# Product-key experts: one product of 512 columns for two of 256, with the halves added by VectorE

## The chip, the cores and the metric

The kernel runs on one core of a Trainium2 chip. The core has five engines that run apart and meet at semaphores: TensorE (PE, matrix products into the eight PSUM banks of 512 columns of float32), VectorE (DVE), ScalarE (ACT), GpSimd (POOL) and SyncE (SP, which here issues the loads). Each engine works through its own instructions strictly in order, and an instruction may wait for a count of a semaphore. The metric is the time of one execution on the device in microseconds; less is better. Inputs, outputs and sums are float32.

## The reference, cut to what matters

The whole program is two transformer blocks: attention of three kinds and product-key experts in the first; a recurrent mixer, latent attention, cross attention and a mixture of experts in the second. The change touches the product-key experts alone:

```python
def peer_ffn(h, w_q, sub1, sub2, u, v):          # h: 256 tokens x 1024
    ...                                          # 8 heads pick 16 of 128 x 128 experts for each token
    expert = jnp.take_along_axis(cand_idx, pos, axis=-1)
    gate = jax.nn.softmax(top_s, axis=-1)
    def step(args):
        x_c, e_c, g_c = args
        a = jnp.einsum('cd,ced->ce', x_c, u[e_c])
        w = jax.nn.gelu(a.astype(jnp.float32), approximate=False).astype(x_c.dtype) * g_c
        return jnp.einsum('ce,ced->cd', w, v[e_c])
```

## The kernel before

The kernel does not gather experts. It walks through all 16384 of them in 128 steps, called keys here, of 128 experts each. For a key it computes the product of the key's `u` (128 experts x 1024) with the input of all 256 tokens, takes gelu, multiplies by a table of gates (zero where a token did not choose the expert), and adds the product with the key's `v` (128 x 1024) to the output, which stays in banks 0 to 3 for all 128 keys.

TensorE gets its operands in a format called fp32r here, which is rounded. To keep precision each operand is split into two parts, high (the rounded value, written by ACT with a copy, `high`) and low (the rest, by DVE with a subtraction, `low`). A product is then three products: high x high, high x low and low x high. The input of the tokens is split once ahead of the loop (`peer_experts`, L1299 to L1313, tiles `peer_input_high` and `peer_input_low`); `u` and `v` of each key in the loop, and the gated values too (`gate`, L1388).

The work of a key n, and who does it:

- SP loads `u` and `v` of the key (512 KB each) into two buffers each (`reload`, L1424). It asks for `v` of key n + 2 when `v_low` of key n is done, and right behind that for `u` of key n + 3, whose condition, `u_low` of key n + 1, is met long before.
- ACT: gelu out of the bank (`act_gelu`, L1364), `v_high`, `u_high`.
- DVE: gate (three operations of 128x256: `gated_high`, `gated`, `gated_low`), `v_low`, `u_low`.
- PE: `pre` (L1328), 8 chunks of 3 matmuls of 256 columns into the first half of one of the banks 4 to 7, and `post` (L1342), 12 matmuls of 512 columns into banks 0 to 3.

The order is written out by hand and shifted, so that engines work on different keys at a time. In its step n PE does `pre` of key n + 2 and then `post` of key n. ACT does gelu of n + 1, `v_high` of n + 1, `u_high` of n + 3 (`act_step`, L1401). DVE does the gate of n + 1, `v_low` of n + 1, `u_low` of n + 3 (`dve_step`, L1413). `v_high` and the gate of a key use buffers that `post` of two keys earlier has read, so they wait for it. A loop (`Fori`) holds four keys in its body, since the banks repeat after four; the first and last four keys stand outside it.

Of the kernel before, what the change touches and what calls it, by code (L numbers as in the profile page):

```python
# [232 lines left out]
class Kernel:  # L233
    def __init__(self, nc, dram, ctx):
# [18 lines left out]
        self.norms_spread = signal("norms_spread")  # L253
        self.scores_ready = signal("scores_ready")
# [1036 lines left out]
def peer_experts(k, gates, raw, hT_keep):  # L1291

    nc = k.nc
    with ExitStack() as c, ExitStack() as c2:
        hT_high, hT_low = (k.sb(f"peer_input_{n}", [P, DC, S], F32R, ctx=c) for n in ("high", "low"))  # L1299

        parts = [[k.sb(f"{m}_{n}", [P, 2, D], F32R, ctx=c) for n in ("high", "low")] for m in "uv"]
        hT = k.sb("peer_input_T_again", [P, DC, S], ctx=c2)
        load_small(k, [(hT[:, :, :], hT_keep)])
        with k.stage() as block:
            @block.scalar
            def _(act):
                nc.scalar.activation(hT_high[:, :, :], hT[:, :, :], ACT.Copy).then_inc(k.act_ready.up(), 1)

            @block.vector
            def _(dve):  # L1310
                dve.wait_ge(k.act_ready.sem, k.act_ready.at(1))
                nc.vector.tensor_tensor(hT_low[:, :, :], hT[:, :, :], hT_high[:, :, :],
                                        ALU.subtract).then_inc(k.dve_step.up(), 1)  # L1313
        c2.close()
        gelu, w = (k.sb(n, [P, 2, S], ctx=c) for n in ("gelu_out", "gated"))
        w_high, w_low = (k.sb(n, [P, 2, S], F32R, ctx=c) for n in ("gated_high", "gated_low"))
        peer_steps(k, gates, raw, parts, hT_high, hT_low, gelu, w, w_high, w_low)

def peer_steps(k, gates, raw, parts, hT_high, hT_low, gelu, w, w_high, w_low):
# [7 lines left out]
    with k.stage() as block:  # L1327
        def pre(pe, n, b, start):  # L1328

            pe.wait_ge(k.u_low_ready.sem, k.u_low_ready.at(n + 1))  # L1330
            if not start:
                pe.wait_ge(k.act_ready.sem, k.act_ready.at(n - 3))
            out = k.ps[:, 4 + b, 0:S]
            for ch in range(DC):
                high, low = (as_u(t, b % 2)[:, ch, :] for t in parts[0])
                h_high, h_low = hT_high[:, ch, :], hT_low[:, ch, :]
                mm(k, out, high, h_high, ch == 0, False)
                mm(k, out, high, h_low, False, False)
                last = mm(k, out, low, h_high, False, ch == DC - 1)
            last.then_inc(k.products.up(), 1)  # L1340
# [23 lines left out]
        def act_gelu(act, n, b, start):  # L1364

            act.wait_ge(k.products.sem, k.products.at(n + 1))
            if not start:
                act.wait_ge(k.weights_gated.sem, k.weights_gated.at(n - 1))
            nc.scalar.activation(gelu[:, b % 2, :], k.ps[:, 4 + b, 0:S], ACT.Gelu).then_inc(k.act_ready.up(), 1)
# [10 lines left out]
        def low(dve, which, n, b):  # L1380
# [5 lines left out]
                                    ALU.subtract).then_inc(ready.up(), 1)  # L1386

# [25 lines left out]
        def dve_step(dve, i, b):  # L1413

            n = TURN * i + b
            if i is not LAST or b + 1 < TURN:
                gate(dve, n + 1, (b + 1) % TURN, i is FIRST and b + 1 < 2)
                low(dve, 1, n + 1, (b + 1) % TURN)
            if i is not LAST or b + 3 < TURN:
                low(dve, 0, n + 3, (b + 3) % TURN)  # L1420

# [41 lines left out]
        def _(dve):  # L1463
            low(dve, 0, 0, 0)
            low(dve, 0, 1, 1)
            gate(dve, 0, 0, True)
            low(dve, 1, 0, 0)
            low(dve, 0, 2, 2)
            for b in range(TURN):
# [4 lines left out]
            for sig in (k.weights_gated, k.u_low_ready, k.v_low_ready):  # L1474
# [1449 lines left out]
```

## Time and profile before

| | |
|---|---|
| Median of 3 runs | 2960.99 us (2958.99 to 2966.97) |
| Profiled execution | 2962.56 us, its span 2960.2 us |
| Busy over the span | PE 2541.0 us (86%), DVE 1119.1 (38%), ACT 662.8 (22%), POOL 124.2 (4%) |
| DMA | 654.58 MB, mean 221 GB/s |
| The 128 keys | `u_low` starts at 560.4 us for the first key; last `v_low` at 1280.9 us |

The times of the trace are those of one execution, and they are counted from the start of its span. The span is what the profiler saw of the engines; the execution's own time is a little longer. The profile names instructions by the line of the kernel and by the tiles that they write and read: `gelu_out<-banks` is gelu. A matmul made by the helper `mm` has line L448, whoever calls it, so the tile names tell `pre` (`peer_input_...`) from `post` (`v_...,gated_...`). The durations of matmuls overlap one another; what a matmul costs in a stream is the distance from its start to the next start. The key loop is a quarter of the program.

### The profile page before, as it was taken

What the parts mean: (1) busy time and instruction counts of PE and PEld (TensorE: products, weight loads), DVE (VectorE), ACT (ScalarE), POOL (GpSimd) and SP (SyncE); (2) the same over time, 40 slices, a digit from 0 to 9 for tenths busy, and PEclk for the clock granted to TensorE, in tenths of its full rate; (3) what the DMA queues carried; (4) which work ended last, traced back from release to release, by engine and by line L of the source; (5) the groups of instructions that cost most, each with busy time, mean ns of one, the idle gap of its engine ahead of it and who ended that gap; (6) DMA issues with size and microseconds to landing.
All of it is one profiled execution on the core that took longest, in us unless ns stands there. A gap on an engine that the chain in (4) does not pass through costs nothing. (4 is left out here: it accounts for less than half of the span.)

```text
span 2960.2 us, 41550 instructions
## 1 busy us (share of the span) xinstructions
PE 2541.0 (86%) x15928; PEld 1797.2 (61%) x15928; DVE 1119.1 (38%) x2354; ACT 662.8 (22%) x1242; POOL 124.2 (4%) x180
## 2 busy tenths in 40 slices
PE   8878886799999999969877699988766867999886
PEld 6537655699999999947744455444335544554442
DVE  1330778666666666624611311111135223111112
ACT  2110018644444444413201100000013011000000
POOL 1120000000000000000200000000002000000000
PEclk9998899999999999989989799999978988999998
DMA  5313320255555555563053299999921523999995
GB/s 191 134 57 130 124 94 35 79 187 190 187 187 184 185 187 188 190 227 135 31 201 127 83 427 426 427 427 428 406 101 37 215 91 149 427 427 426 427 427 246
DMA packets 130873, 654.58 MB, mean 221 GB/s; under 512 B 15523, under 2 KB 25126, under 8 KB 95782
## 3 DMA queue, kind: packets, MB, share of 16 engines
q1 hardware_dynamic: 117504, 625.64, 53.4%
q10 hardware_dynamic: 13238, 27.10, 2.6%
q8 instruction: 94, 1.54, 0.2%
q14 instruction: 37, 0.30, 0.0%
HBM read 643.92 MB, written 8.78 MB: 220 GB/s over the span
## 5 line engine op out<-in xcount | busy, mean ns | idle before, releaser
L448 PE MATMUL banks<-weight_ring,window_rows_T 128*64 128x256 f32 x2496 | 286.9, 384 | 44.0 <-DMA weight_ring<-in_moe_w_up 29.8
L448 PE MATMUL banks<-peer_input_high,u_high 128*128 128x256 f32 x1024 | 290.5, 284 | 14.2 <-DVE u_low L1385 14.1
L448 PE MATMUL banks<-peer_input_high,u_low 128*128 128x256 f32 x1024 | 290.7, 284 | 0.0
L448 PE MATMUL banks<-peer_input_low,u_high 128*128 128x256 f32 x1024 | 290.6, 284 | 0.0
L448 PEld LDWEIGHTS banks<-weight_ring,window_rows_T 128*64 128x64 f32 x2496 | 188.7, 138 | 156.3 <-DMA weight_ring<-in_moe_w_up 41.2
L2678 DVE COPY expert_hidden_T<-banks 128x256 f32<-128x256 f32 x64 | 27.2, 425 | 676.9 <-PE banks L2540 676.9
L448 PEld LDWEIGHTS banks<-peer_input_high,u_high 128*128 128x128 f32 x1024 | 197.0, 192 | 20.2 <-DVE u_low L1385 15.1
L448 PE MATMUL banks<-v_high,gated_high 128*128 128x512 f32 x512 | 200.9, 392 | 0.0
L448 PE MATMUL banks<-v_low,gated_high 128*128 128x512 f32 x512 | 200.7, 392 | 0.0
L448 PEld LDWEIGHTS banks<-peer_input_low,u_high 128*128 128x128 f32 x1024 | 197.0, 192 | 4.7
L448 PE MATMUL banks<-v_high,gated_low 128*128 128x512 f32 x512 | 199.2, 389 | 0.0
L448 PE MATMUL banks<-more_weight_slots,window_rows_T 128*64 128x256 f32 x1600 | 181.2, 381 | 19.5 <-DMA more_weight_slots<-in_moe_w_up 16.0
L448 PEld LDWEIGHTS banks<-peer_input_high,u_low 128*128 128x128 f32 x1024 | 197.0, 192 | 0.0
L1385 DVE TENSOR_TENSOR u_low<-u_of_key,u_high 128x1024 fp32r<-128x1024 f32 x128 | 156.8, 1226 | 95.8 <-ACT u_high L1377 95.3
L1377 ACT ACTIVATE v_high<-v_of_key 128x1024 fp32r<-128x1024 f32 x128 | 135.7, 1060 | 254.6 <-PE banks L448 254.6
L2647 ACT ACTIVATE expert_outputs<-banks 128x512 f32<-128x512 f32 x64 | 38.2, 597 | 622.0 <-PE banks L448 622.0
L448 PEld LDWEIGHTS banks<-more_weight_slots,window_rows_T 128*64 128x64 f32 x1600 | 118.5, 137 | 89.3 <-DMA more_weight_slots<-in_moe_w_up 22.4
L1377 ACT ACTIVATE u_high<-u_of_key 128x1024 fp32r<-128x1024 f32 x128 | 135.6, 1060 | 137.9 <-DMA u_of_key<-in_peer_u_T 130.1
L1385 DVE TENSOR_TENSOR v_low<-v_of_key,v_high 128x1024 fp32r<-128x1024 f32 x128 | 155.9, 1218 | 0.0
L448 PE MATMUL banks<-weight_ring,expert_hidden_T 128*64 128x512 f32 x672 | 153.5, 598 | 1.2 <-DVE expert_hidden_T L2678 1.2
L2556 PE MATMUL banks<-expert_outputs,gate_of_window_row 64*128 64x512 f32 x512 | 127.2, 615 | 1.9 <-ACT expert_outputs L2647 1.9
L1394 DVE TENSOR_TENSOR gated_high<-gelu_out,gates 128x256 fp32r<-128x256 f32 x128 | 54.4, 425 | 169.3 <-PE banks L448 164.6
(454 smaller groups left out, 3522.5 us busy)
## 6 DMA issues: line engine op xcount, KB each, us to landing
weight_ring<-in_moe_w_down SPq DMA_DIRECT2D x42, 2048.0 KB, 35.4
weight_ring<-in_moe_w_gate SPq DMA_DIRECT2D x40, 2048.0 KB, 35.4
weight_ring<-in_moe_w_up SPq DMA_DIRECT2D x38, 2048.0 KB, 34.5
u_of_key<-in_peer_u_T SPq DMA_DIRECT2D x128, 512.0 KB, 4.5
v_of_key<-in_peer_v_rows SPq DMA_DIRECT2D x128, 512.0 KB, 3.5
more_weight_slots<-in_moe_w_up SPq DMA_DIRECT2D x26, 2048.0 KB, 33.2
more_weight_slots<-in_moe_w_gate SPq DMA_DIRECT2D x24, 2048.0 KB, 34.9
more_weight_slots<-in_moe_w_down SPq DMA_DIRECT2D x22, 2048.0 KB, 35.4
```

Source lines behind the costliest of these rows:

```text
L448: return k.nc.tensor.matmul(out, lhsT, rhs, start=start, stop=stop)
L1377: nc.scalar.activation(parts[which][0][:, b % 2, :], raw[which][:, b % 2, :], ACT.Copy).then_inc(ready.up(), 1)
L1385: nc.vector.tensor_tensor(part_low[:, b % 2, :], raw[which][:, b % 2, :], part_high[:, b % 2, :], ALU.subtract).then_inc(ready.up(), 1)
L1394: nc.vector.tensor_tensor(w_high[:, b % 2, :], gelu[:, b % 2, :], g, ALU.mult).then_inc(k.dve_step.up(), 1)
L2556: last = k.nc.tensor.matmul(k.ps[:, 2 * tt + dh, :], share[half, tt * P:(tt + 1) * P], outs[half, :], start=start, stop=stop, skip_group_c ...
L2647: nc.scalar.activation(b.outs[:, e % 2, :], k.ps[:, DOWN_BANK, :], ACT.Copy).then_inc(k.act_evacuated.up(), 1)
L2678: nc.vector.tensor_copy(b.hid_T[:, e % 2, :, :].rearrange("p m n -> p (m n)"), k.ps[:, TURN_BANK, 0:2 * P]).then_inc(k.turned_copied.up(), 1)
```

## The change

Three things change together.

The two parts of the input now lie side by side in one tile, `peer_input_high_low`, 2 x 256 columns for each chunk. In `pre` one matmul of 512 columns multiplies `u_high` with both parts, into both halves of the bank, and one of 256 columns adds `u_low` with the high part to the first half. That is 16 matmuls where there were 24, with the same number of columns.

The value of the key is now the sum of the two halves of the bank. DVE makes it (`add`): a copy of the second half to a new tile `key_sums`, and, when that is done, an addition of the first half to it. gelu reads `key_sums` and waits for this addition and not for PE, and `pre` of four keys later waits for the addition and not for gelu before it writes the bank again.

In DVE's step the order changes from gate, `v_low`, `u_low` to `v_low`, gate, `u_low`, `add`, the last for key n + 2.

```diff
--- before.py
+++ after.py
@@ -251,6 +251,8 @@
         self.rows_turned = signal("rows_turned")
         self.row_sums = signal("row_sums")
         self.norms_spread = signal("norms_spread")
+        self.halves_copied = signal("halves_copied")
+        self.key_sums_ready = signal("key_sums_ready")
         self.scores_ready = signal("scores_ready")
         self.scores_read = signal("scores_read")
         self.shift_ready = signal("shift_ready")
@@ -1296,7 +1298,8 @@
 
     nc = k.nc
     with ExitStack() as c, ExitStack() as c2:
-        hT_high, hT_low = (k.sb(f"peer_input_{n}", [P, DC, S], F32R, ctx=c) for n in ("high", "low"))
+        hT_both = k.sb("peer_input_high_low", [P, DC, 2, S], F32R, ctx=c)
+        hT_high, hT_low = (hT_both[:, :, n, :] for n in range(2))
 
         parts = [[k.sb(f"{m}_{n}", [P, 2, D], F32R, ctx=c) for n in ("high", "low")] for m in "uv"]
         hT = k.sb("peer_input_T_again", [P, DC, S], ctx=c2)
@@ -1304,19 +1307,19 @@
         with k.stage() as block:
             @block.scalar
             def _(act):
-                nc.scalar.activation(hT_high[:, :, :], hT[:, :, :], ACT.Copy).then_inc(k.act_ready.up(), 1)
+                nc.scalar.activation(hT_high, hT[:, :, :], ACT.Copy).then_inc(k.act_ready.up(), 1)
 
             @block.vector
             def _(dve):
                 dve.wait_ge(k.act_ready.sem, k.act_ready.at(1))
-                nc.vector.tensor_tensor(hT_low[:, :, :], hT[:, :, :], hT_high[:, :, :],
+                nc.vector.tensor_tensor(hT_low, hT[:, :, :], hT_high,
                                         ALU.subtract).then_inc(k.dve_step.up(), 1)
         c2.close()
-        gelu, w = (k.sb(n, [P, 2, S], ctx=c) for n in ("gelu_out", "gated"))
+        gelu, w, total = (k.sb(n, [P, 2, S], ctx=c) for n in ("gelu_out", "gated", "key_sums"))
         w_high, w_low = (k.sb(n, [P, 2, S], F32R, ctx=c) for n in ("gated_high", "gated_low"))
-        peer_steps(k, gates, raw, parts, hT_high, hT_low, gelu, w, w_high, w_low)
-
-def peer_steps(k, gates, raw, parts, hT_high, hT_low, gelu, w, w_high, w_low):
+        peer_steps(k, gates, raw, parts, hT_both, total, gelu, w, w_high, w_low)
+
+def peer_steps(k, gates, raw, parts, hT_both, total, gelu, w, w_high, w_low):
 
     nc = k.nc
     as_u = lambda t, b: t[:, b, :].rearrange("p (c e) -> p c e", c=DC)
@@ -1329,14 +1332,14 @@
 
             pe.wait_ge(k.u_low_ready.sem, k.u_low_ready.at(n + 1))
             if not start:
-                pe.wait_ge(k.act_ready.sem, k.act_ready.at(n - 3))
-            out = k.ps[:, 4 + b, 0:S]
+                pe.wait_ge(k.key_sums_ready.sem, k.key_sums_ready.at(n - 3))
+            out = k.ps[:, 4 + b, :]
             for ch in range(DC):
                 high, low = (as_u(t, b % 2)[:, ch, :] for t in parts[0])
-                h_high, h_low = hT_high[:, ch, :], hT_low[:, ch, :]
-                mm(k, out, high, h_high, ch == 0, False)
-                mm(k, out, high, h_low, False, False)
-                last = mm(k, out, low, h_high, False, ch == DC - 1)
+                nc.tensor.matmul(out, high, hT_both[:, ch, :, :].rearrange("p a t -> p (a t)"), start=ch == 0, stop=False,
+                                 skip_group_check=True)
+                last = nc.tensor.matmul(out[:, 0:S], low, hT_both[:, ch, 0, :], start=False, stop=ch == DC - 1,
+                                        skip_group_check=True)
             last.then_inc(k.products.up(), 1)
 
         def post(pe, n, b, first_one, last_one):
@@ -1363,10 +1366,10 @@
 
         def act_gelu(act, n, b, start):
 
-            act.wait_ge(k.products.sem, k.products.at(n + 1))
+            act.wait_ge(k.key_sums_ready.sem, k.key_sums_ready.at(n + 1))
             if not start:
                 act.wait_ge(k.weights_gated.sem, k.weights_gated.at(n - 1))
-            nc.scalar.activation(gelu[:, b % 2, :], k.ps[:, 4 + b, 0:S], ACT.Gelu).then_inc(k.act_ready.up(), 1)
+            nc.scalar.activation(gelu[:, b % 2, :], total[:, b % 2, :], ACT.Gelu).then_inc(k.act_ready.up(), 1)
 
         def high(act, which, n, i, b, start):
 
@@ -1384,6 +1387,16 @@
             part_high, part_low = parts[which]
             nc.vector.tensor_tensor(part_low[:, b % 2, :], raw[which][:, b % 2, :], part_high[:, b % 2, :],
                                     ALU.subtract).then_inc(ready.up(), 1)
+
+        def add(dve, n, b, start):
+
+            dve.wait_ge(k.products.sem, k.products.at(n + 1))
+            if not start:
+                dve.wait_ge(k.act_ready.sem, k.act_ready.at(n - 1))
+            nc.vector.tensor_copy(total[:, b % 2, :], k.ps[:, 4 + b, S:2 * S]).then_inc(k.halves_copied.up(), 1)
+            dve.wait_ge(k.halves_copied.sem, k.halves_copied.at(n + 1))
+            nc.vector.tensor_tensor(total[:, b % 2, :], k.ps[:, 4 + b, 0:S], total[:, b % 2, :],
+                                    ALU.add).then_inc(k.key_sums_ready.up(), 1)
 
         def gate(dve, n, b, start):
 
@@ -1414,10 +1427,12 @@
 
             n = TURN * i + b
             if i is not LAST or b + 1 < TURN:
+                low(dve, 1, n + 1, (b + 1) % TURN)
                 gate(dve, n + 1, (b + 1) % TURN, i is FIRST and b + 1 < 2)
-                low(dve, 1, n + 1, (b + 1) % TURN)
             if i is not LAST or b + 3 < TURN:
                 low(dve, 0, n + 3, (b + 3) % TURN)
+            if i is not LAST or b + 2 < TURN:
+                add(dve, n + 2, (b + 2) % TURN, i is FIRST and b + 2 < 2)
 
         @block.sync
         def _(sp):
@@ -1463,15 +1478,17 @@
         def _(dve):
             low(dve, 0, 0, 0)
             low(dve, 0, 1, 1)
+            add(dve, 0, 0, True)
             gate(dve, 0, 0, True)
             low(dve, 1, 0, 0)
             low(dve, 0, 2, 2)
+            add(dve, 1, 1, True)
             for b in range(TURN):
                 dve_step(dve, FIRST, b)
             with dve.Fori(1, LAST) as i:
                 for b in range(TURN):
                     dve_step(dve, i, b)
-            for sig in (k.weights_gated, k.u_low_ready, k.v_low_ready):
+            for sig in (k.weights_gated, k.u_low_ready, k.v_low_ready, k.halves_copied, k.key_sums_ready):
                 sig.repeated(turns - 2, TURN)
             k.dve_step.repeated(turns - 2, 2 * TURN)
             for b in range(TURN):
```

DVE's instructions of one step in the body of the loop, before. REGISTER_ALU and ISA rows are work of the sequencer with counters and addresses.

```order
L1394 ISA [waits down_products,act_ready]
L1394 TENSOR_TENSOR gated_high<-gelu_out,gates 128x256
L1396 TENSOR_TENSOR gated<-gelu_out,gates 128x256
L1397 ISA
L1398 TENSOR_TENSOR gated_low<-gated,gated_high 128x256 [waits dve_step]
L1385 TENSOR_TENSOR v_low<-v_of_key,v_high 128x1024 [waits v_high_ready]
L1383 REGISTER_ALU
L1385 TENSOR_TENSOR u_low<-u_of_key,u_high 128x1024 [waits u_high_ready]
```

The same step in the changed kernel:

```order
L1388 TENSOR_TENSOR v_low<-v_of_key,v_high 128x1024 [waits v_high_ready]
L1407 ISA [waits down_products,act_ready]
L1407 TENSOR_TENSOR gated_high<-gelu_out,gates 128x256
L1409 TENSOR_TENSOR gated<-gelu_out,gates 128x256
L1410 ISA
L1411 TENSOR_TENSOR gated_low<-gated,gated_high 128x256 [waits dve_step]
L1386 REGISTER_ALU
L1388 TENSOR_TENSOR u_low<-u_of_key,u_high 128x1024 [waits u_high_ready]
L1393 REGISTER_ALU
L1396 COPY key_sums<-banks 128x256 [waits act_ready,products]
L1398 TENSOR_TENSOR key_sums<-banks,key_sums 128x256 [waits halves_copied]
```

`v_low` stands ahead of the gate, and copy and addition close the step; they wait for the product (`products`) and for gelu of two keys earlier, which has read the same buffer (`act_ready`).

ACT's instructions in the body of the loop, before, from gelu of one key to gelu of the next:

```order
L1369 ACTIVATE gelu_out<-banks 128x256 [waits weights_gated]
L1377 ACTIVATE v_high<-v_of_key 128x1024 [waits down_products,v_landed_0]
L1373 ISA
L1377 ACTIVATE u_high<-u_of_key 128x1024 [waits products,u_landed_0]
L1454 REGISTER_ALU
L1454 COMPARE_AND_BRANCH
L1369 ACTIVATE gelu_out<-banks 128x256 [waits weights_gated,products]
```

And in the changed kernel:

```order
L1372 ACTIVATE gelu_out<-key_sums 128x256 [waits weights_gated,key_sums_ready]
L1380 ACTIVATE v_high<-v_of_key 128x1024 [waits down_products,v_landed_0]
L1376 ISA
L1379 REGISTER_ALU [waits u_landed_0]
L1380 ACTIVATE u_high<-u_of_key 128x1024 [waits products]
L1469 REGISTER_ALU
L1469 COMPARE_AND_BRANCH
L1372 ACTIVATE gelu_out<-key_sums 128x256 [waits weights_gated,key_sums_ready]
```

The order on ACT is the same; what gelu waits for is another engine's signal, with `v_high` and `u_high` queued behind it as before.

## Rows read from the trace of the kernel before

**Rows 1.** Table of windows: window, length; busy PE, PEld, DVE, ACT, POOL (count), PEclk, DMA, GB/s

```profile
561.00:1285.00 724.00, 722.13 (x4608) 658.30 (x4608) 453.04 (x640) 311.95 (x384) 0.00 (x0) 1.00 0.51 183
```

**Rows 2.** Waits, window 580 to 1270: who waited for whom, us, times, longest

```profile
ACT v_high L1377 <- PE banks L448: 248.7, 123, 2.4
DVE gated_high L1394 <- PE banks L448: 159.6, 123, 1.9
ACT u_high L1377 <- DMA u_of_key<-in_peer_u_T: 125.4, 119, 1.8
DVE u_low L1385 <- ACT u_high L1377: 91.4, 119, 1.5
```

**Rows 3.** Timeline of PE: start us, duration us, instruction

```profile
1001.34 0.40 PE L448 MATMUL banks<-v_high,gated_high 128*128 128x512 f32 x1
...
1004.09 0.28 PE L448 MATMUL banks<-peer_input_high,u_high 128*128 128x256 f32 x1
...
1006.96 0.40 PE L448 MATMUL banks<-v_high,gated_high 128*128 128x512 f32 x1
```

**Rows 4.** Timeline of DVE, one key

```profile
1004.46 0.43 DVE L1394 TENSOR_TENSOR gated_high<-gelu_out,gates 128x256 fp32r<-128x256 f32 x1 [1.66 <-PE banks L448]
1004.81 0.42 DVE L1396 TENSOR_TENSOR gated<-gelu_out,gates 128x256 f32<-128x256 f32 x1
1005.26 0.43 DVE L1398 TENSOR_TENSOR gated_low<-gated,gated_high 128x256 fp32r<-128x256 f32 x1
1005.60 1.22 DVE L1385 TENSOR_TENSOR v_low<-v_of_key,v_high 128x1024 fp32r<-128x1024 f32 x1
1008.07 1.23 DVE L1385 TENSOR_TENSOR u_low<-u_of_key,u_high 128x1024 fp32r<-128x1024 f32 x1 [1.25 <-ACT u_high L1377]
```

**Rows 5.** Groups of instructions by shape, whole program: busy us, mean ns

```profile
L2678 DVE COPY expert_hidden_T<-banks 128x256 f32<-128x256 f32 x64 | 27.2, 425 | 676.9 <-PE banks L2540 676.9
L2657 DVE TENSOR_TENSOR expert_hidden<-silu_out,banks 128x256 f32<-128x256 f32 x64 | 26.3, 410 | 18.2 <-PE banks L448 18.2
L916 DVE SCALAR_TENSOR_TENSOR queries_T<-queries_T,columns,banks 128x256 f32<-128x256 f32 x8 | 3.7, 480 | 9.8 <-PE banks L448 9.8
L1369 ACT ACTIVATE gelu_out<-banks 128x256 f32<-128x256 f32 x128 | 48.0, 375 | 18.0 <-PE banks L448 16.7
L1817 ACT ACTIVATE rw_gate_low<-rw_gate_low 128x256 f32<-128x256 f32 x1 | 0.4, 416 | 0.0
```

**Rows 6.** Timeline, operations back to back on ACT and on DVE

```profile
566.93 0.38 ACT L1369 ACTIVATE gelu_out<-banks 128x256 f32<-128x256 f32 x1 [4.34 <-PE banks L448]
567.21 1.05 ACT L1377 ACTIVATE v_high<-v_of_key 128x1024 fp32r<-128x1024 f32 x1
...
1270.04 1.22 DVE L1385 TENSOR_TENSOR v_low<-v_of_key,v_high 128x1024 fp32r<-128x1024 f32 x1
1271.17 1.22 DVE L1385 TENSOR_TENSOR u_low<-u_of_key,u_high 128x1024 fp32r<-128x1024 f32 x1
```

**Rows 7.** Timeline of ACT, two splits of `u`

```profile
1006.98 1.06 ACT L1377 ACTIVATE u_high<-u_of_key 128x1024 fp32r<-128x1024 f32 x1 [1.57 <-DMA u_of_key<-in_peer_u_T]
...
1011.57 1.06 ACT L1377 ACTIVATE u_high<-u_of_key 128x1024 fp32r<-128x1024 f32 x1 [0.54 <-DMA u_of_key<-in_peer_u_T]
```

**Rows 8.** Timeline, a DVE result awaited by ACT

```profile
59.74 0.41 DVE L907 TENSOR_SCALAR head_norms<-banks 16x256 f32<-16x256 f32 x1 [3.88 <-PE banks L448]
...
60.19 0.42 ACT L953 ACTIVATE head_norms<-head_norms 16x256 f32<-16x256 f32 x1 [0.60 <-DVE head_norms L907]
```

**Rows 9.** Timeline of SyncE's DMA queue (SPq): when loads are issued

```profile
1001.24 0.33 SPq L1289 DMA_DIRECT2D v_of_key<-in_peer_v_rows  x1
1002.26 0.33 SPq L1289 DMA_DIRECT2D u_of_key<-in_peer_u_T  x1
1006.85 0.33 SPq L1289 DMA_DIRECT2D v_of_key<-in_peer_v_rows  x1
1007.37 0.33 SPq L1289 DMA_DIRECT2D u_of_key<-in_peer_u_T  x1
```

## Prediction

> **What bounds the kernel now.** I took the stretch of the key loop first, since the change touches nothing else. The table of windows [rows 1] gives 724 us for 128 keys: TensorE (PE) is busy for 722.13 of them at a granted clock of 1.00 (the 2.4 GHz level), VectorE (DVE) for 453.04, ScalarE (ACT) for 311.95. The list of waits [rows 2] says the same from the other side: ACT and DVE wait for PE, ACT for a transfer of `u`, DVE for ACT, and no line of it has PE waiting. So PE sets the pace. The timeline of PE [rows 3] gives the pace: `post` of a key starts at 1001.34, the next `pre` at 1004.09, the next `post` at 1006.96. That is 2.75 us for 12 matmuls of 512 columns (0.229 each), 2.87 us for 24 of 256 columns (0.1196 each), 5.62 us a key. DVE's row of one key [rows 4] must be read for starts, not durations: an operation of 0.42 to 0.43 us is followed after 0.35, one that waits for its predecessor's result after 0.45.
>
> **The change on PE.** Columns a key stay as they are: 24 x 256 before, 8 x 512 + 8 x 256 now, so what goes is what a matmul costs beyond its columns. A chunk took 3 x 0.1196 = 0.359 us and takes 0.229 + 0.120 = 0.349: 0.010 less, over 8 chunks 0.08. `pre` goes to 2.79, a key to 5.54 us. If PE still set the pace this would be worth 0.08 x 127 = 10 us.
>
> The Trainium skill, page "TensorE: Matmul & The Clock Gate", section "Back-to-back issue gap", gives a fixed 2.5 ns on top of the columns of each matmul at 2.4 GHz. By it the 8 matmuls saved would be worth 20 ns a key, some 2.5 us in all (an estimate from that page), and not 10; this trace has its 256-column matmuls at 119.6 ns where the page's formula gives 109, and its 512-column ones at 229 where it gives 216.
>
> **The change on DVE and ACT.** DVE gets two operations a key: a copy of 128x256 out of the bank and an addition of 128x256 with one input in the bank. The gate and `v_low` change places, and gelu on ACT now waits for the addition and no longer for PE. By busy time there is room: 3.54 us a key of DVE (453.04 / 128) plus 0.425 for the copy and 0.41 for the addition [rows 5] is 4.37 of 5.54. But the order of the queues closes a ring, and a ring must be summed. ACT issues gelu of a key, then `v_high` of the same key behind it. DVE begins its step with `v_low` of that key, which waits for `v_high`; then gate, `u_low` and, last, copy and addition of the next key; gelu of the next key waits for that addition. One turn of the ring is one key. From start to start:
>
> - gelu to `v_high`, back to back on ACT: 0.28 with gelu reading the bank [rows 6]. An activation of this size that reads SBUF takes 0.416 where gelu takes 0.375 [rows 5], so I take 0.03 more: 0.31.
> - `v_high` to `v_low`: as `u_high` at 1006.98 to `u_low` at 1008.07, 1.09 [rows 4, 7].
> - `v_low` to gate: 1.13, as two splits back to back on DVE [rows 6].
> - gate to `u_low`: as 1004.46 to 1005.60, 1.14 [rows 4].
> - `u_low` to copy: 1.13 again. The product it reads has ended by then.
> - copy to addition, with a wait for its own result: as `gated` to `gated_low`, 0.45 [rows 4].
> - addition to gelu: 0.41, and 0.04 from a DVE result to the ACT operation that waits for it (59.74 + 0.41 to 60.19) [rows 8]: 0.45.
>
> Sum: 0.31 + 1.09 + 1.13 + 1.14 + 1.13 + 0.45 + 0.45 = 5.70 us. This is longer than PE's 5.54. DVE would sit idle about 1.5 us in it, at the one place where it waits for ACT, and neither engine can use this time. In the kernel before, gelu waited for PE alone and the ring did not exist.
>
> **The transfer in the ring.** SyncE's queue is not edited, but it follows `v_low`: it issues the load of `v` 1.25 us after `v_low` starts, then the next load of `u` after 0.52 or 1.02 us in turn, and `u_high` starts 4.20 or 4.72 us later [rows 4, 7, 9]. From `v_low` of key n to `u_high` of key n + 3 it is 5.97 or 6.99 us, the long one for each second key. That gives a second ring, over two keys: 6.99, then `u_high` to `u_low` 1.09, to copy 1.13, to addition 0.45, to gelu 0.45, to `v_high` 0.31, to `v_low` of key n + 2 1.09: 11.51 us, or 5.755 a key. With 5.97 it would be 5.25 and not count. So the longest ring is the one with the slow transfer, 0.055 above the other. With the old order of gate and `v_low`, `v_low` could not start before gelu + 0.42 + 0.03 and the gate's 1.14, 1.59 in the place of 0.31 + 1.09, and this ring would be 5.85: the swap is worth 0.1 us here, and that is in the 5.755.
>
> PE then waits 5.755 - 5.54 = 0.2 us a key, before `pre`, for `u_low`. That is too little idle time to expect another clock level in view of the 1.00 held here.
>
> **The sum.** 5.755 - 5.62 = 0.135 us a key, over 126 keys 17 us, and about 1 us at the start, where copy and addition stand ahead of the first gate with nothing beside them: 18. The split of the input ahead of the loop is the same two operations on another layout, at nothing. Everything behind the loop starts later by the same amount, and its work is not touched. The profiled execution took 2962.56 us (span 2960.2 and 2.4 around it), which becomes 2980.6; it stands 1.6 above the median of the runs, so the forecast against the median 2960.99 is 2979.
>
> **Bounds of what the trace does not show.** Copy and addition out of the bank: the nearest rows are 0.425 and 0.41, and I take them; the far one is the fused operation of this size with a bank input, 0.48 [rows 5]. Both at 0.48 make the first ring 5.82 a key, 26 us in all. Both shorter by 0.02 and gelu still at 0.28 leave 5.63 in the first ring and 5.72 in the second, plus 13 us. The landing of `u`: 0.1 us less brings the second ring to 5.705, plus 11; 0.25 more brings it to 5.88, plus 33; 0.35 more to 5.93, plus 40. The cheap ends together leave 5.63 to 5.65, plus 2 to 5; the dear ends together reach plus 45.
>
> **Rivals.**
> 1. The ring is shorter than I sum and PE keeps the pace: faster. All of PE's saving is then real: 5.54 a key, 10 us less, 2951. It decides at a ring of 5.54, so 0.16 us would have to be missing in seven steps, three of which are measured on the very same instructions. For it speaks only DVE's low share of 63%. Chance 0.06.
> 2. Ring and PE nearly cancel: copy, addition and gelu at the cheap end and `u` landing 0.1 to 0.2 us sooner, 5.63 to 5.69 a key, less than 9 us more, about 2966. Chance 0.14.
> 3. The transfer is what is late: in a step of another phase `u` lands 0.2 to 0.35 us later than now, and the second ring goes to 5.85 to 5.93: plus 29 to 40 us, about 2995. For it speaks that ACT already waits for this transfer in nearly every key, 125.4 us over 119 times [rows 2]. Chance 0.18.
> 4. The change does not shorten `pre` (a 512-column product over both halves at more than 0.229): PE at 5.62 or a little over. It changes nothing as long as the ring is the longer one; it is inside my forecast.
>
> My own case, the ring at 5.72 to 5.84 a key and 2974 to 2990, has 0.60; what is left, 0.02, is beyond these. The range that holds 8 in 10 is 2964 to 3004. A difference of 0.3%, 9 us, is about what a measurement of this kernel can tell from none: faster by more 0.06, within it 0.14, slower by more 0.80.
>
> **What would show it.** In the profile after: 5.7 to 5.8 us from `post` to `post`; PE's first matmul of a key waiting for `u_low`, 0.1 to 0.3 us each time; gelu waiting for `key_sums` on DVE and no longer for PE, over 100 times; `v_low` waiting for `v_high` by more than 1 us a key; DVE waiting for PE nearly nowhere; `u_low` waiting for `u_high` in each second key at most. Inside `pre`, pairs of matmuls 0.349 apart. I am wrong in the mechanism if `post` to `post` is 5.54 and PE has no wait, wrong in the size if copy or addition take over 0.45, and rival 3 has it if the keys whose `u_low` waits for `u_high` are the late ones by more than 0.2 us.

## The result and the profile after

The changed kernel takes 2986.9 us (median of 4 runs, 2985.75 to 2988.79), the kernel before 2959.99 in its runs beside it. The ratio is 1.0088, 95% interval 1.0069 to 1.0106: slower by 26.9 us, where I had forecast 18 and a range of 2964 to 3004.

The table of windows over the 128 keys, the columns as in [rows 1]. The stretch is 749 us long where it was 724:

```profile
561.00:1310.00 749.00, 739.17 (x3584) 594.84 (x3583) 541.97 (x895) 309.31 (x383) 0.00 (x0) 0.99 0.50 177
```

PE has 3584 matmuls where it had 4608; DVE is busy 542 us where it was 453. By busy time nothing is full but PE, and its overlapping matmuls read as 739 of 749 us although it now waits in most keys. The list of waits (window 580 to 1290; who waited for whom: us, times, longest) shows who waits for whom:

```profile
ACT gelu_out L1372 <- DVE key_sums L1398: 311.5, 122, 3.5
DVE v_low L1388 <- ACT v_high L1380: 178.9, 123, 1.8
ACT u_high L1380 <- DMA u_of_key<-in_peer_u_T: 99.6, 115, 1.7
PEld banks L1339 <- DVE u_low L1388: 31.9, 91, 0.7
PEld banks L1339 <- issue: 14.0, 30, 0.6
PE banks L1339 <- DVE u_low L1388: 1.9, 9, 0.3
DVE u_low L1388 <- ACT u_high L1380: 1.6, 7, 0.4
```

Against [rows 2] the roles are reversed. ACT and DVE waited for PE; now ACT waits for DVE and DVE for ACT, each once a key, and PE (through its weight loads, PEld) waits for `u_low`. Two engines that wait for each other once a turn are a ring. Here is one turn of it in the timelines (start us, duration us). DVE first, to be held against [rows 4]:

```profile
1002.13 1.23 DVE L1388 TENSOR_TENSOR v_low<-v_of_key,v_high 128x1024 fp32r<-128x1024 f32 x1 [1.43 <-ACT v_high L1380]
1003.27 0.42 DVE L1407 TENSOR_TENSOR gated_high<-gelu_out,gates 128x256 fp32r<-128x256 f32 x1
...
1004.41 1.22 DVE L1388 TENSOR_TENSOR u_low<-u_of_key,u_high 128x1024 fp32r<-128x1024 f32 x1
1005.54 0.42 DVE L1396 COPY key_sums<-banks 128x256 f32<-128x256 f32 x1
1005.99 0.43 DVE L1398 TENSOR_TENSOR key_sums<-banks,key_sums 128x256 f32<-128x256 f32 x1
1007.85 1.22 DVE L1388 TENSOR_TENSOR v_low<-v_of_key,v_high 128x1024 fp32r<-128x1024 f32 x1 [1.43 <-ACT v_high L1380]
...
1010.23 1.22 DVE L1388 TENSOR_TENSOR u_low<-u_of_key,u_high 128x1024 fp32r<-128x1024 f32 x1
```

and ACT's part of it:

```profile
1000.73 0.42 ACT L1372 ACTIVATE gelu_out<-key_sums 128x256 f32<-128x256 f32 x1 [2.20 <-DVE key_sums L1398]
1001.06 1.04 ACT L1380 ACTIVATE v_high<-v_of_key 128x1024 fp32r<-128x1024 f32 x1
...
1006.45 0.42 ACT L1372 ACTIVATE gelu_out<-key_sums 128x256 f32<-128x256 f32 x1 [2.51 <-DVE key_sums L1398]
1006.78 1.04 ACT L1380 ACTIVATE v_high<-v_of_key 128x1024 fp32r<-128x1024 f32 x1
1009.14 1.06 ACT L1380 ACTIVATE u_high<-u_of_key 128x1024 fp32r<-128x1024 f32 x1 [1.32 <-DMA u_of_key<-in_peer_u_T]
```

Read it as a chain of starts: gelu 1000.73, `v_high` + 0.33, `v_low` + 1.07, gate + 1.14, `u_low` + 1.14, copy + 1.13, addition + 0.45, gelu + 0.46: 5.72 us. The next turn took 5.83 from `v_low` to `v_low` (1007.85 to 1013.68): its `u_low` started at 1010.23, right after `u_high` had ended at 1010.20, where the gate would have let it start 0.10 earlier. That is the late transfer; the load had been issued at 1004.40 and `u_high` started 4.74 later:

```profile
1003.39 0.33 SPq L1291 DMA_DIRECT2D v_of_key<-in_peer_v_rows  x1
1004.40 0.33 SPq L1291 DMA_DIRECT2D u_of_key<-in_peer_u_T  x1
```

From one start of `v_low` to the next, by the timeline, every second key takes 5.72 or 5.80, the others 5.72 to 6.09, and the mean over 108 keys in the middle is 5.79 us (5.62 before).

### The profile page after: what moved, and what is told of

It is laid out like the page before. It is cut to its first block and busy times, and to the rows that moved or that the text cites. A ratio compares the mean times of both kernels' runs of the same rounds, so it can differ in the third digit from the quotient of the medians.

```text
span 2984.3 us, 40004 instructions
## 1 busy us (share of the span) xinstructions
PE 2559.2 (86%) x14904; PEld 1735.0 (58%) x14904; DVE 1209.4 (41%) x2610; ACT 660.9 (22%) x1242; POOL 123.8 (4%) x180
## 5 line engine op out<-in xcount | busy, mean ns | idle before, releaser
L1339 PE MATMUL banks<-peer_input_high_low,u_high 128*128 128x512 f32 x1024 | 381.5, 412 | 19.8 <-DVE u_low L1388 17.1
L1341 PE MATMUL banks<-peer_input_high_low,u_low 128*128 128x256 f32 x1024 | 289.0, 282 | 0.0
L1339 PEld LDWEIGHTS banks<-peer_input_high_low,u_high 128*128 128x128 f32 x1024 | 193.9, 189 | 103.5 <-DVE u_low L1388 48.0
L1341 PEld LDWEIGHTS banks<-peer_input_high_low,u_low 128*128 128x128 f32 x1024 | 195.3, 191 | 0.1
L1372 ACT ACTIVATE gelu_out<-key_sums 128x256 f32<-128x256 f32 x128 | 53.5, 418 | 329.5 <-DVE key_sums L1398 329.5
L450 PE MATMUL banks<-h_T_gain_bias,weight_ring 128*128 128x256 f32 x480 | 108.7, 388 | 3.9 <-PEq L346 3.9
L450 PEld LDWEIGHTS banks<-v_high,gated_high 128*128 128x128 f32 x512 | 96.3, 188 | 23.0 <-issue 1.4
```

The costliest lines, as they stand in the source:

```text
L450: return k.nc.tensor.matmul(out, lhsT, rhs, start=start, stop=stop)
L1339: nc.tensor.matmul(out, high, hT_both[:, ch, :, :].rearrange("p a t -> p (a t)"), start=ch == 0, stop=False, skip_group_check=True)
L1341: last = nc.tensor.matmul(out[:, 0:S], low, hT_both[:, ch, 0, :], start=False, stop=ch == DC - 1, skip_group_check=True)
L1372: nc.scalar.activation(gelu[:, b % 2, :], total[:, b % 2, :], ACT.Gelu).then_inc(k.act_ready.up(), 1)
```

## The experiments

Each kernel ran beside the kernel before on one chip, and the ratio is from those runs; the kernel before had medians of 2959.45 to 2960.46 us in them. The changed kernel was not run again beside them, so a difference from it is one between occasions, good to one or two us. The last column is the mean distance of two starts of `v_low` over the same 108 keys of the trace.

| kernel | median us | ratio to before, 95% | us a key |
|---|---|---|---|
| before | 2960 | 1 | 5.620 |
| changed | 2986.9 | 1.0069 to 1.0106 | 5.791 |
| e1 `v_high` ahead of gelu | 2962.75 | 0.9998 to 1.0016 | 5.592 |
| e2 gate ahead of `v_low` | 3002.7 | 1.013 to 1.0161 | 5.921 |
| e3 `u` asked for earlier | 2979.27 | 1.0054 to 1.0085 | 5.738 |
| e4 products alone | 2955.95 | 0.9976 to 0.9994 | 5.590 |
| e5 three products, halves | 2987.5 | 1.0082 to 1.0113 | 5.792 |
| e6 one copy more | 3020.68 | 1.0195 to 1.0226 | 6.070 |
| e7 one reduction | 2972.95 | 1.0029 to 1.006 | 5.671 |
| e8 e7 and e3 | 2962.6 | 0.9997 to 1.0015 | 5.593 |
| e10 e7, e3, e1, old order | 2962.03 | 0.9997 to 1.0015 | 5.585 |
| e11 before, `post` in halves | 2975.86 | 1.0039 to 1.0067 | 5.760 |

My theory is the two rings of the prediction. The rivals: PE's own wide products are slow; DVE's added work costs by its amount; the transfer is all there is.

**e1: cut the ring on ACT.** In `act_step`:

```diff
-                act_gelu(act, n + 1, b1, i is FIRST and b + 1 < 2)
                 high(act, 1, n + 1, i1, b1, i is FIRST and b + 1 < 2)
+                act_gelu(act, n + 1, b1, i is FIRST and b + 1 < 2)
```

> The changed kernel with v_high ahead of gelu in ACT's step; all work is kept. Ring theory (gelu, v_high, v_low, gate, u_low, copy, addition, and gelu again, 5.72 us a key): v_high no longer stands behind gelu, the ring is cut to gelu, gate, u_low, copy, addition (3.6 us), and PE sets the pace at 8 x 0.3505 + 12 x 0.2295 = 5.56 us a key: 6 to 8 us below the kernel before, some 33 below the changed one, with no wait of v_low for an ACT operation that itself waited for DVE. If PE's own products were what is slow in the changed kernel, it stays at 5.79 a key and 26 us above the kernel before. If DVE's added work costs by its amount, wherever it stands, it stays slower too.

Measured: 5.59 us a key and 2962.75, 24 us below the changed kernel. All of DVE's added work is still there. Its longest waits (window 580 to 1280):

```profile
ACT v_high L1380 <- PE banks L450: 311.2, 126, 4.2
DVE v_low L1388 <- ACT v_high L1380: 151.1, 126, 2.4
```

gelu no longer waits for `key_sums`, `v_high` waits for PE as in [rows 2], and no line has PE waiting. Swapping two instructions on ACT removed 0.2 us a key. That rules out the rival of the wide products and the one of DVE's amount of work. I missed the total by 10 us: I had expected 6 to 8 below the kernel before and got 3 above, which the interval does not tell from the same. Some 4 of that is the pace (5.59 and not 5.56, see e4). Some 3 lie at the loop's ends: the last matmul starts 5.1 us after the last `v_low` (3.9 in the kernel before), and the first keys cost 1.6 us more than the pace accounts for (why, stands under "The sum" below). The stretches ahead of and behind the loop were 0.7 and 1.5 us longer in this trace. The rest I cannot place.

**e2: the old order on DVE.** The gate stands ahead of `v_low` again, all else as changed:

```diff
-                low(dve, 1, n + 1, (b + 1) % TURN)
                 gate(dve, n + 1, (b + 1) % TURN, i is FIRST and b + 1 < 2)
+                low(dve, 1, n + 1, (b + 1) % TURN)
```

> The changed kernel with DVE's step in the old order, gate before v_low. Theory of two rings: v_low starts later in the step (gelu + 0.45 + the gate's 1.14 = 1.59 instead of 0.33 + 1.08 = 1.41), so v_low asks for the loads later and the ring over two keys that contains the transfer of u grows by 0.18, to 5.85 to 5.9 a key: 8 to 12 us above the changed kernel, 34 to 38 above the kernel before. If only the ring over one key counted, cutting v_low out of it would give 5.56 a key and a gain; if PE were the bound, no change.

Measured: 5.92 a key, 16 us above the changed kernel, so on the side of two rings and somewhat beyond its size. The turns now alternate between 4.9 and 6.6 to 7.4 us, and the first three lines of the waits (window 580 to 1280) name the transfer:

```profile
ACT gelu_out L1372 <- DVE key_sums L1398: 275.4, 118, 2.7
ACT u_high L1380 <- DMA u_of_key<-in_peer_u_T: 139.8, 61, 3.7
DVE u_low L1388 <- ACT u_high L1380: 114.8, 60, 3.3
```

`u_low` waits for `u_high` in every second key, 60 times, up to 3.3 us. The short turn of 4.9 is the first ring without `v_high` in it: from gelu to the gate 0.56, then 1.14 to `v_low`, 1.13 to `u_low`, 1.13 to the copy, 0.45 to the addition and 0.46 to gelu, or 0.54 in each fourth key. What it wins is given back in the next, since the two-key ring sets the sum. I had taken 0.45 from gelu to the gate that waits for it; the 0.11 more, once in two keys, is 0.055 a key and most of what lies between the 5.85 of my sum and 5.92.

**e3: take the transfer out.** SP asks for `u` of key n + 3 before it waits for `v_low` of key n (`load_u` and `load_v` are the two halves of `reload`; their definitions are left out here):

```diff
-            with sp.Fori(0, PK // 2 - 1) as i:
-                for b in range(2):
-                    reload(2 * i + b, b)
+            load_u(0, 0)
+            load_u(1, 1)
+            load_v(0, 0)
+            with sp.Fori(1, PK // 2 - 1) as i:
+                load_u(2 * i, 0)
+                load_v(2 * i - 1, 1)
+                load_u(2 * i + 1, 1)
+                load_v(2 * i, 0)
+            load_v(PK - 3, 1)
```

> The changed kernel with SP's queue in another order: the load of u of key n + 3 is issued ahead of the load of v of key n + 2 and no longer waits behind v_low. Two rings: the transfer leaves the ring, u_high follows v_high at once, the ring over one key is left with 5.72 (5.80 each fourth key), mean 5.74: 4 to 8 us below the changed kernel, still 16 to 22 above the kernel before. If the transfer is all that makes the changed kernel slow, it goes to or below the kernel before. If it has no part in it, nothing changes.

Measured: 5.738 a key, 7.6 us below the changed kernel, 20 above the one before. The turns are 5.72, 5.72, 5.72, 5.80 through the whole loop, and the waits (window 580 to 1280) have two lines of ACT and DVE left, none with a transfer:

```profile
ACT gelu_out L1372 <- DVE key_sums L1398: 417.3, 122, 3.5
DVE v_low L1388 <- ACT v_high L1380: 179.4, 123, 2.1
```

So the first ring is 5.72 by itself, and the transfer adds 0.053 a key: it is not all there is. The 5.80 comes once in the loop's body of four keys. In the changed kernel's timeline it stands between addition and gelu, 0.53 where it is 0.46 otherwise:

```profile
1017.55 0.42 DVE L1398 TENSOR_TENSOR key_sums<-banks,key_sums 128x256 f32<-128x256 f32 x1
...
1018.08 0.42 ACT L1372 ACTIVATE gelu_out<-key_sums 128x256 f32<-128x256 f32 x1 [3.03 <-DVE key_sums L1398]
```

In one of the four keys the program has the wait for `key_sums` on a register instruction ahead of gelu, and gelu itself is issued only after it. That this is where the 0.07 comes from fits its place and its count; no run took it away.

**e4: PE's part alone.** The wide products as changed, gelu reads the first half of the bank and waits for PE, no copy, no addition, DVE in its old order. It leaves out the product of `u_high` with the low part of the input.

```diff
-            act.wait_ge(k.key_sums_ready.sem, k.key_sums_ready.at(n + 1))
+            act.wait_ge(k.products.sem, k.products.at(n + 1))
...
-            if i is not LAST or b + 2 < TURN:
-                add(dve, n + 2, (b + 2) % TURN, i is FIRST and b + 2 < 2)
...
```

> The 512-column products alone: 8 x (512 + 256) columns in pre as in the changed kernel, but gelu reads the first half of the bank and waits for PE, DVE adds nothing and has its old order. It leaves out the product of u_high with the low part of the input. This is PE's part of the change by itself: 0.3505 a pair, 5.56 a key against 5.62, 7 to 9 us below the kernel before. By a fixed cost of only 2.5 ns a matmul it would be 2.5 us below. If the wide products themselves were slow, it is slower than the kernel before.

Measured: 3.5 us below the kernel before, 5.590 a key. `pre` went from 2.873 to 2.809 us on average (2.79 forecast), and `post`, whose instructions did not change, from 2.748 to 2.781. So the saving on PE is real and a third of what I had: `pre` gave most of it, and `post` took half of that back. Why `post` takes 0.03 longer behind the wide `pre` is not settled; it does so in e1, e8 and e10 too.

**e5: the other part alone.** Halves and additions stay, the wide product is undone:

```diff
-                nc.tensor.matmul(out, high, hT_both[:, ch, :, :].rearrange("p a t -> p (a t)"), start=ch == 0, stop=False,
+                nc.tensor.matmul(out[:, 0:S], high, hT_both[:, ch, 0, :], start=ch == 0, stop=False,
+                                 skip_group_check=True)
+                nc.tensor.matmul(out[:, S:2 * S], high, hT_both[:, ch, 1, :], start=False, stop=False,
                                  skip_group_check=True)
```

> The changed kernel with its wide product undone: u_high times the high part goes into the first half of the bank and u_high times the low part into the second half, two matmuls of 256 columns; the halves are still added by VectorE and the order is the changed one. PE needs 5.62 us a key, less than the rings. Ring theory: no difference from the changed kernel, 5.77 to 5.81 us a key, 24 to 29 us above the kernel before. If the wide product has a part in the loss or in a hidden gain, the time moves by 4 us or more from the changed kernel's.

Measured: 5.792 a key and 2987.5, the changed kernel's numbers. With PE off the ring, a `pre` of 24 matmuls or of 16 gives the same time. The whole loss is in how the sum is made, none in the product.

**e6: one copy more in the ring.**

```diff
+            nc.vector.tensor_copy(more[:, b % 2, :], k.ps[:, 4 + b, S:2 * S])
             nc.vector.tensor_copy(total[:, b % 2, :], k.ps[:, 4 + b, S:2 * S])
```

> The changed kernel with one copy more of 128x256 out of the bank, to a tile nobody reads, ahead of the copy in DVE's step. It occupies DVE 0.34 us from start to start. Ring theory: the ring over one key goes from 5.74 to 6.08 and is then longer than the one with the transfer (which takes half of the 0.34 a key, 5.96): 6.08 us a key, 34 to 38 us above the changed kernel, and u_low no longer waits for u_high. If DVE's work counts by its amount only, DVE has 1.4 us idle a key and it costs nothing. If only the ring with the transfer counted, half: 20 us.

Measured: 33.8 us above the changed kernel (34 to 38 expected), 6.070 a key (6.08 expected). Turns of 6.05, each fourth 6.13, so 0.33 on the first ring: an operation that nobody waits for costs its full distance from start to start. And `u_low` has no line of waiting for `u_high` any more; the longest four of the list (window 580 to 1280):

```profile
ACT gelu_out L1372 <- DVE key_sums L1399: 356.8, 115, 3.7
DVE v_low L1388 <- ACT v_high L1380: 168.5, 116, 1.5
ACT u_high L1380 <- DMA u_of_key<-in_peer_u_T: 56.1, 66, 1.2
PEld banks L1339 <- DVE u_low L1388: 54.0, 84, 0.8
```

**e7: shorten the ring.** One reduction for copy and addition:

```diff
-            nc.vector.tensor_copy(total[:, b % 2, :], k.ps[:, 4 + b, S:2 * S]).then_inc(k.halves_copied.up(), 1)
-            dve.wait_ge(k.halves_copied.sem, k.halves_copied.at(n + 1))
-            nc.vector.tensor_tensor(total[:, b % 2, :], k.ps[:, 4 + b, 0:S], total[:, b % 2, :],
-                                    ALU.add).then_inc(k.key_sums_ready.up(), 1)
+            nc.vector.tensor_reduce(total[:, b % 2, :], k.ps[:, 4 + b, :].rearrange("p (a t) -> p t a", a=2),
+                                    AX, ALU.add).then_inc(k.key_sums_ready.up(), 1)
```

> The changed kernel with one reduction over the two halves of the bank (512 elements in, 256 out) in the place of copy and addition. By operations of 512 elements from a bank at 0.69 us it saves 0.18 from the start of the copy to gelu. Ring theory: ring over one key 5.72 - 0.18 = 5.54, ring with the transfer 5.82 - 0.09 in its two-key mean, so 5.66 to 5.72 us a key: 10 to 16 us below the changed kernel, 10 to 16 above the kernel before. If a strided read of the bank is slow, it is slower than the changed kernel.

Measured: 14 us below the changed kernel, 5.671 a key. The row of the reduction in the groups by shape:

```profile
L1396 DVE TENSOR_REDUCE key_sums<-banks 128x256 f32<-128x512 f32 x128 | 87.5, 684 | 4.4 <-PE banks L1341 4.4
```

0.684 us for 512 elements. In the kernel before a copy of 512 elements out of a bank without a stride takes 0.691 (`probs_T`), so the stride costs nothing here. The short turns are 5.53, 0.19 less than before; those with the late transfer go up to 6.1.

**e8: shorten one ring and take the other out.** e7 and e3 together.

> The reduction of e7 and the earlier request for u of e3 together. The ring with the transfer is gone, the ring over one key is 5.54 (5.62 each fourth key), below PE's 5.59 as measured with the products alone. Ring theory: PE sets the pace again, 5.58 to 5.60 us a key, v_high waits for PE and no longer for gelu, and the total is within 4 us of the kernel before. If the rings are not what counts, it stays above by 10 us or more.

Measured: 5.593 a key, all turns of the middle between 5.58 and 5.61, and 2962.6 us, within what can be told from the kernel before. One detail came out otherwise: I had expected `v_high` to wait for PE in the list, and it has one line of 1.1 us. gelu comes 5.53 after gelu by the ring and PE's `post` ends at almost the same moment; `v_high` starts 0.37 after gelu where it is 0.33 when only the queue holds it, and 0.49 after the last matmul of `post` starts, as in the kernel before. So it is the wait for PE, too short to be listed.

```profile
583.30 0.42 ACT L1372 ACTIVATE gelu_out<-key_sums 128x256 f32<-128x256 f32 x1 [3.21 <-DVE key_sums L1396]
583.67 1.06 ACT L1380 ACTIVATE v_high<-v_of_key 128x1024 fp32r<-128x1024 f32 x1
```

The list of e8 holds a warning. It has the same two lines of mutual waits as the changed kernel, gelu for `key_sums` with 403.4 us and `v_low` for `v_high` with 191.2, and yet PE sets the pace in it. Two engines that wait for each other show that a ring exists. That it is the longest is shown by its sum against PE's work, and by PE waiting in the list.

**e10: all repairs, to beat both kernels.** One reduction, `u` earlier, `v_high` ahead of gelu, and the gate ahead of `v_low` again.

> The changed kernel with all four repairs: one reduction for copy and addition, u asked for earlier, v_high ahead of gelu on ACT, and the gate ahead of v_low on DVE again. Both rings are cut and the end of the loop is the old one (the last gate no longer stands behind the last v_low, 1.2 us). PE sets the pace at 5.59 us a key, 0.03 below the kernel before, 3.8 us in all; the start costs 1 to 2 us more. So 0 to 4 us below the kernel before, 2956 to 2960, and 1 to 3 us below the versions with two or one repairs. If the rest above the kernel before came from elsewhere than the ends of the loop, it stays at 2962.

Measured: 5.585 a key, the best of the complete kernels, and 2962.03 us, not below the kernel before (ratio 0.9997 to 1.0015) and above the 2956 to 2960 that I had expected. The end of the loop is the old one again, 3.9 us from the last `v_low` to the last matmul. But the first keys cost 2.5 us more than the pace accounts for, and from the first `u_low` to the last matmul it is 722.5 us against 724.4 before: of 4 us in the pace 2 are left. The stretches ahead of and behind the loop were 2.3 and 0.9 us longer in this trace, which is more than that. No complete version beats the kernel before; e4, which does, leaves out a product.

**e11: what a matmul costs beyond its columns, from the other side.** The kernel before, with `post` in 24 matmuls of 256 columns:

```diff
-                for half in range(2):
-                    cols = slice(half * 512, (half + 1) * 512)
-                    out = k.ps[:, 2 * tt + half, :]
+                for q in range(4):
+                    cols = slice(q * 256, (q + 1) * 256)
+                    out = k.ps[:, 2 * tt + q // 2, q % 2 * 256:(q % 2 + 1) * 256]
```

> The kernel before, with the 12 matmuls of 512 columns in post made 24 of 256; columns, sums and waits stay. 48 matmuls a key for 36. It prices a matmul beyond its columns from the other side. By the products-alone experiment (8 matmuls fewer took 0.030 us off a key) it is 3.75 ns each: 0.045 a key, 5.665, plus 5 to 7 us. By the distances inside the kernel before (0.229 for 512 columns, 0.1196 for 256, as my prediction had it) it is 12 x 0.010 = 0.12 a key, 5.74, plus 15 us. By 2.5 ns a matmul it is 0.03 a key, plus 4 us.

Measured: 15.4 us above the kernel before, 5.760 a key, 0.14 for 12 matmuls; `post` itself went from 2.748 to 2.880. That is near the size by the distances of the kernel before (0.12), and three times the 0.045 by the price that e4 gave for a matmul. The same price does not hold in both directions.

## Why the prediction was right, and where its sizes were off

**The bound before** was PE, at 5.62 us a key. Right: e11 lengthens PE's work alone, by 0.14 us a key, and the time went up by 15.4.

**The ring on ACT and DVE.** Forecast 5.70, found 5.72 in the changed kernel and in e3, with 5.80 in each fourth key. Step by step: gelu to `v_high` 0.33 (0.31), `v_high` to `v_low` 1.07 (1.09), `v_low` to gate 1.14 (1.13), gate to `u_low` 1.14 (1.14), `u_low` to copy 1.13 (1.13), copy to addition 0.45 (0.45), addition to gelu 0.46 (0.45). gelu reading SBUF takes 0.42 us, as the row of 0.416 [rows 5] said. Missing was the fourth key's 0.07 to 0.08, 0.02 a key, 2.5 us in all; the order of ACT's instructions showed such a register instruction with a wait, and I gave it no price. PE's wait, which I had at 0.1 to 0.3 us each time, is 0.35 on the list (31.9 us over 91 times), and the granted clock stayed at 1.00 between 600 and 1200 us, as I had taken it.

**The transfer.** Forecast + 0.055 a key, measured 5.791 - 5.738 = 0.053. The place was right, every second key, but that the mean fits so well is partly luck. My ring had each of these keys late by the same 0.11 us; in the middle of the trace `u_low` starts late in 37 of 54 of them, by 0.03 to 0.36 us, and on time in the others. That the swap of gate and `v_low` helps here was right too: 0.13 a key by e2 (0.1 forecast).

**PE.** The saving was mis-sized: 0.03 us a key (e4), 3.5 us, where I had 0.08 and 10. Inside `pre` the eight matmuls gave back 0.064, or 8 ns each where I had 10; the 0.033 that `post` grew by I had put at nothing. This term did not enter the forecast, only rival 1. The Trainium skill's 2.5 ns a matmul ("TensorE: Matmul & The Clock Gate", "Back-to-back issue gap"), by which I had estimated 2.5 us, came nearer to the total of e4. But the 8 ns inside `pre` do not bear it out, and for e11 the same rule would give 4 us, an estimate from that page, where 15.4 were measured. Neither rule gives both. Inside `pre` the pairs are 0.35 apart as forecast, but the first matmul after a wait is 0.33 from the second and not 0.23:

```profile
1005.68 0.50 PE L1339 MATMUL banks<-peer_input_high_low,u_high 128*128 128x512 f32 x1
1006.01 0.28 PE L1341 MATMUL banks<-peer_input_high_low,u_low 128*128 128x256 f32 x1
1006.13 0.40 PE L1339 MATMUL banks<-peer_input_high_low,u_high 128*128 128x512 f32 x1
1006.36 0.28 PE L1341 MATMUL banks<-peer_input_high_low,u_low 128*128 128x256 f32 x1
```

so that `pre` takes 2.92 where the ring holds it up. It costs nothing there.

**The sum.** I had 17 us for 126 keys and 1 for the start. The trace has (5.791 - 5.620) x 126 = 21.5 for the keys. Counted from the first `u_low` of the loop (559.28 us here, 560.38 before), the first `v_low` comes 0.85 us later than in the kernel before, close to the 1 that I had. But I had given no price to what this does to PE. `u_low` of the third key comes 0.84 later too, so PE is idle for longer ahead of `pre` of this key, 2.18 us where it was 1.12 (before, then changed):

```profile
570.89 0.39 PE L448 MATMUL banks<-peer_input_high,u_high 128*128 128x256 f32 x1 [1.12 <-DVE u_low L1385]
...
570.64 0.50 PE L1339 MATMUL banks<-peer_input_high_low,u_high 128*128 128x512 f32 x1 [2.18 <-DVE u_low L1388]
```

and in the 3 us from 572 to 575 its granted clock is 0.50, the 1.2 GHz level, where it was 1.00 (columns as in [rows 1]; before, then changed):

```profile
572.00:575.00 3.00, 3.00 (x22) 2.81 (x22) 1.11 (x1) 0.51 (x1) 0.00 (x0) 1.00 0.83 291
...
572.00:575.00 3.00, 3.00 (x11) 2.53 (x10) 2.16 (x4) 1.49 (x2) 0.00 (x0) 0.50 0.52 209
```

From its first matmul to its last this `pre` takes 4.0 us where it took 2.85. In e4, which adds nothing on DVE, it takes 2.82 at a clock of 1.00. In the eight kernels that make the sum on DVE beside this one it takes 3.9 to 4.3, except in e7, where it takes 2.81; no run was made to separate the idle time from the rest. From the first `u_low` to the eleventh `v_low` the start costs 1.8 us more than the pace accounts for, the 0.85 included.

At the end of the loop the last keys give back 0.8 us, and the last matmul starts 5.1 us after the last `v_low` and not 3.9, since the gate now stands behind `v_low` and the last `post` waits for it, a place I had not looked at; with the old order, in e2 and e10, it is 3.9 again. From the first `u_low` to the last matmul it is 748.3 us where it was 724.4, 23.8 more and not 18: 4.5 of the difference are the pace, 0.8 the start and 0.4 the end.

The part behind the loop is 1.4 us longer and the part ahead of it 1.1 shorter. The part behind holds unchanged instructions and lies between 1673 and 1678 us over all kernels here, so I read no cause into either. The span went from 2960.2 to 2984.3, 24.1; the medians differ by 26.9, and the remaining 3 lie between one profiled execution and the medians.

**Rival 1**, the gain, did not happen; by e1, e8 and e10 it does once the rings are cut, at 5.585 to 5.593 a key, but nothing of it reaches the total. **Rival 2**, less than 9 us more, is out by the 26.9. **Rival 3**, a transfer that lands later, did not come: the load of `u` has its median of 4.5 us from issue to landing as before. **Rival 4** is out by e4, where `pre` is shorter by 0.064 us; e5 shows that it would have changed nothing, as I had written.

## What to carry to other kernels

When a change makes one engine's early instruction wait for another engine's last one, follow the queues in both directions and add up the starts: busy shares of 72% and 41% hid a ring that was longer than the bound engine's work. The list of mutual waits finds such a ring, but only the sum tells whether it is the longest (e8). Where such a ring sets the pace, everything in it costs its full distance, also an operation that nobody reads (e6), and the cheapest repair is to move an instruction that need not be in it ahead of the one that waits (e1). A transfer that is requested at a point of the ring makes a second ring, here over two turns.

## What the runs showed that I had not expected

Making 12 matmuls of 512 columns into 24 of 256 cost 0.14 us a key, 11 ns each inside `post`. Making 16 of 256 into 8 of 512 gave back 8 ns each inside `pre`, but only 0.03 us a key in all, since `post` changed its duration with unchanged instructions: 2.748 us in the kernel before, 2.781 in e4. What does this is open.

A delay of 0.84 us on another engine at the start of the loop came with a larger one on PE: it was idle for 1.1 us longer, behind this wait its granted clock fell to the 1.2 GHz level, and one `pre` took 1.15 us longer. That the longer wait is the reason for the clock is not shown.
